# A chunk-pipelined mixer layer: the next chunk's x is loaded, measured, published and normalised at other steps

## What is computed

```
mod = silu(c) @ w_ada + b_ada;  shift, scale, gate = split(mod, 3)
h = layer_norm(x) * (1 + scale) + shift
proj = h @ w_in                                   # (2048,1024) @ (1024,2560)
xa, ga, u, v, gb = split(proj)                    # 512 channels each
ya = pool_mixer(xa) * silu(ga)                    # causal means over 2,4,8,16 tokens, a 128x128 map per group
yb = sgu_mixer(gelu(u), gelu(v)) * silu(gb)       # per 128 tokens and head: u * (W LN(v) + b)
y = concat(ya, yb) @ w_out                        # (2048,1024) @ (1024,1024)
z = alpha * x + gate * y
return layer_norm(z) * ln_g + ln_b
```

## Time and profile before

| what | value |
|---|---|
| three runs | 684.82, 684.26, 682.94 us, median 684.26 |
| profiled execution | 681.78 us, of which the span is 680.1 us |
| granted PE clock, mean | 0.990 |
| PE busy | 656.3 us (97%) |
| DVE busy | 496.2 us (73%) |
| ACT busy | 252.3 us (37%) |
| DMA queues of SP and ACT | 58.6% and 13.7% of 16 engines |

### The profile page before, as it was taken

The page is one execution under the profiler, slowest core; times in us unless marked ns, Lnnn a source line. Parts: engine busy times, 40 slices in busy tenths (PEclk is TensorE's granted clock), DMA queues, the critical chain, the costliest instruction groups (busy, mean ns, idle before and its releaser), DMA issues.

```text
span 680.1 us, 8503 instructions
## 1 busy us (share of the span) xinstructions
PE 656.3 (97%) x3055; PEld 546.0 (80%) x3055; DVE 496.2 (73%) x980; ACT 252.3 (37%) x335; POOL 51.1 (8%) x77
## 2 busy tenths in 40 slices
PE   8999999999989999989899999999999999999995
PEld 8888888877868888877688888888788888888884
DVE  5678897839979969539997757649997653436776
ACT  4424543316511332233673333242673332333300
POOL 2000100100002210000001210000001210000010
PEclk9999999998999999999899999999999999999999
DMA  8999776989399895997448995897549885654111
GB/s 337 359 344 360 260 280 249 287 217 355 102 323 379 289 409 195 215 347 275 153 157 288 320 314 178 147 371 270 161 149 315 299 317 193 207 166 141 64 63 62
DMA packets 52987, 168.62 MB, mean 248 GB/s; under 512 B 8621, under 2 KB 9681, under 8 KB 52946
## 3 DMA queue, kind: packets, MB, share of 16 engines
q1 hardware_dynamic: 44306, 136.63, 58.6%
q10 hardware_dynamic: 8640, 31.46, 13.7%
HBM read 139.75 MB, written 28.32 MB: 247 GB/s over the span
## 4 chain that ended last, share of the span: by engine, by line
PE 65%; DVE 15%; DMA 10%; issue 5%; ACT 3%; SPq 1%; ACTq 0%; POOL 0%; POOLq 0%; DVEq 0%
PE bank_b L1331 43%; PE bank_a L1331 16%; DMA w_float<-in_w_units 4%; DMA w_float<-xa_units 2%; DVE w_low L841 2%; DVE x_norm L868 2%; DMA token_rows<-x_rstd 2%; PE bank_a L1418 1%; PE bank_a L1458 1%; DMA out_units<-mod_spare 1%; PE bank_b L1391 1%; PE bank_a L1449 1%; ACT w_high L677 1%; DVE y_low L1064 1%; DVE mixed L1245 1%
## 5 line engine op out<-in xcount | busy, mean ns | idle before, releaser
L1331 PE MATMUL bank_b<-h_high,w_high 128*128 128x512 f32 x512 | 202.5, 395 | 2.2 <-issue 2.0
L1331 PE MATMUL bank_b<-h_high,w_low 128*128 128x512 f32 x512 | 199.6, 390 | 0.0
L1331 PE MATMUL bank_b<-h_low,w_high 128*128 128x512 f32 x512 | 199.5, 390 | 0.0
L677 ACT ACTIVATE w_high<-w_float 128x1024 fp32r<-128x1024 f32 x98 | 103.3, 1055 | 136.4 <-DMA w_float<-in_w_units 87.7
L1331 PEld LDWEIGHTS bank_b<-h_high,w_high 128*128 128x128 f32 x512 | 96.3, 188 | 22.5 <-issue 3.5
L1331 PEld LDWEIGHTS bank_b<-h_high,w_low 128*128 128x128 f32 x512 | 96.2, 188 | 20.0
L1331 PEld LDWEIGHTS bank_b<-h_low,w_high 128*128 128x128 f32 x512 | 96.3, 188 | 19.5 <-issue 0.5
L841 DVE TENSOR_TENSOR w_low<-w_float,w_high 128x1024 fp32r<-128x1024 f32 x38 | 46.3, 1220 | 12.8 <-ACT w_high L677 12.6
L613 POOL TENSOR_TENSOR z_rstd<-z_var_eps,minus_half 128x1 f32<-128x1 f32 x16 | 19.0, 1185 | 406.2 <-DVE z_var_eps L1162 199.4
L1331 PE MATMUL bank_a<-w_high,y_high 128*128 128x512 f32 x96 | 39.1, 408 | 7.4 <-DVE w_low L841 7.4
L1331 PE MATMUL bank_a<-w_high,h_high 128*128 128x512 f32 x96 | 38.1, 397 | 2.8 <-DVE tanh L1154 2.8
(11 more groups left out here) (223 smaller groups left out, 1037.1 us busy)
## 6 DMA issues: line engine op xcount, KB each, us to landing
w_float<-in_w_units SPq DMA_DIRECT2D x74, 512.0 KB, 5.3
w_low<-low_units ACTq DMA_DIRECT2D x60, 512.0 KB, 4.9
x_norm<-in_x SPq DMA_DIRECT2D x16, 512.0 KB, 6.3
low_units<-w_low SPq DMA_DIRECT2D x16, 512.0 KB, 7.7
z<-in_x SPq DMA_DIRECT2D x16, 512.0 KB, 6.0
w_float<-out_units SPq DMA_DIRECT2D x16, 512.0 KB, 4.1
out<-z SPq DMA_DIRECT2D x15, 512.0 KB, 6.3
z<-in_mod_units SPq DMA_DIRECT2D x12, 512.0 KB, 9.6
```

The lines of the kernel that those rows point to most:

```text
L677: nc.scalar.activation(w_of(c, n)[0], w_float(c, n), ACT.Copy).then_inc(w_high, 1)
L1331: last = mm(bank, wl if n == 2 else wh, ml if n == 1 else mh, start=start and n == 0, stop=stop and n == 2, skip_group_check=skip_group_check)
```

## The change

In chunks 1 and 2 the x tiles are loaded at steps 1 to 4 (6 to 9 before), measured at 5 to 8 (8 to 11), the rows stored at 9 (12), and the eight blocks normalised over steps 13 to 19 (two at each of 16 to 19). In chunk 0 the loads stay, the last two tiles are measured at 12 and 13 (14 and 15), and the rows stored at 14 (16). In every chunk the fetch of the rows stands three steps behind their store (one before), and chunk 0 too issues one x-by-channel load a step (four at once before). `sum_weights(1)` moves from the last step of chunk 0 to the first of chunk 1, and its stores one step on. No instruction is added or removed on PE, DVE, ACT or GpSimd. Nor is any DMA.

```diff
-SUMS_IN = {(0, 24): 0, (0, 27): 1, (1, 4): 2, (1, 9): 3}
-PREP_STORE_IN = {(0, 25): 0, (1, 1): 1, (1, 6): 2, (1, 11): 3}
+SUMS_IN = {(0, 24): 0, (1, 0): 1, (1, 4): 2, (1, 9): 3}
+PREP_STORE_IN = {(0, 25): 0, (1, 2): 1, (1, 6): 2, (1, 11): 3}
...
-FAST_X_ROWS_IN = 12
-FAST_X_CENTRE_IN = {16: (0, 1), 17: (2, 3), 18: (4, 5), 19: (6, 7)}
+FAST_X_ROWS_IN = 9
+FAST_X_CENTRE_IN = {13: (0,), 14: (1, 2), 15: (3,), 16: (4,), 17: (5,), 18: (6,), 19: (7,)}
+ROWS_BACK = 3
...
-                    if not last and 6 <= n < 6 + TILES:
-                        j = n - 6
+                    if not last and x_load_in(c) <= n < x_load_in(c) + TILES:
+                        j = n - x_load_in(c)
                         sp.wait_ge(h_high, (c + 1) * KT)
                         sp.dma_start(xn[:, j, :], x_tiles[c + 1, j]).then_inc(xn_landed[j], 16)
...
                     if not last and x_rows_in <= n < x_rows_in + TILES:
-                        for i in (n - x_rows_in,) if c in FAST else (range(TILES) if n == x_rows_in else ()):
-                            sp.dma_start(xT[:, 2 * i:2 * i + 2, :], x_channels[c + 1][:, 2 * i:2 * i + 2, :])\
-                                .then_inc(xT_landed[i], 16)
-                    if not last and n == x_rows_in + 1:
+                        i = n - x_rows_in
+                        sp.dma_start(xT[:, 2 * i:2 * i + 2, :], x_channels[c + 1][:, 2 * i:2 * i + 2, :])\
+                            .then_inc(xT_landed[i], 16)
+                    if not last and n == x_rows_in + ROWS_BACK:
                         sp.wait_ge(rows_stored, (c + 1) * 32)
```

More of the change, by code:

```diff
@@ L73 @@
 QUARTER = 256
-X_STATS_IN = {10: 0, 11: 1, 14: 2, 15: 3}
-X_ROWS_IN = 16
+X_LOAD_IN = 6
+X_STATS_IN = {10: 0, 11: 1, 12: 2, 13: 3}
+X_ROWS_IN = 14
 X_CENTRE_IN = {19: (0, 1), 20: (2, 3), 21: (4, 5), 22: (6, 7)}
 H_IN = {20: (0, 1), 21: (2, 3), 22: (4, 5), 23: (6, 7)}
-FAST_X_STATS_IN = {8: 0, 9: 1, 10: 2, 11: 3}
-FAST_X_ROWS_IN = 12
-FAST_X_CENTRE_IN = {16: (0, 1), 17: (2, 3), 18: (4, 5), 19: (6, 7)}
+FAST_X_LOAD_IN = 1
+FAST_X_STATS_IN = {5: 0, 6: 1, 7: 2, 8: 3}
+FAST_X_ROWS_IN = 9
+FAST_X_CENTRE_IN = {13: (0,), 14: (1, 2), 15: (3,), 16: (4,), 17: (5,), 18: (6,), 19: (7,)}
+ROWS_BACK = 3
 FAST_H_IN = {22: (0,), 23: (1,), 24: (2,), 26: (3,), 28: (4,), 29: (5,), 30: (6,), 32: (7,)}
@@ L380, in x_tables, with x_load_in @@
             return X_STATS_IN, X_ROWS_IN, X_CENTRE_IN, H_IN
+        def x_load_in(c):
+            return FAST_X_LOAD_IN if c in FAST else X_LOAD_IN
         def m_sem(m):
```

## The result

The changed kernel takes 668.65 us (668.01 to 669.73, four runs), the kernel before beside it 684.54 us (682.94 to 686.13, four runs): ratio 0.977, 95% interval 0.974 to 0.980. Forecast were 666.0 us and a range of 662.5 to 673.0. The profiled execution takes 668.01 us, of which the span is 666.3 (before 681.78 and 680.1).

The account below looks back on a forecast made before the run. PE was busy 97% of the span, so only idling and clock could be won: 4.7 + 3.9 + 2.0 + 6.5 + 2.0 = 19.1, less 1.0 = 18.1 us, giving 663.7 profiled, 666 as median; range 662.5 to 673.

Parts of the forecast that it names:

- The list of places: Seven PE idle records behind the set-up, in chunks 0 to 2, taken as all that can be won: 19.1 us.
- B: Start of chunk 1: 2.82 us of PE idling and 1.89 of clock, to go by moving the sums; 4.71 us.
- A: Between units 19 and 20 of chunk 0: 2.17 us of PE idling, 1.7 of clock, to go; 3.9 us.
- The hiding work: Chunk 1's start: five units of PE work (27 us) against some 20 of DVE cover DVE's 3 us lateness.
- C: Ahead of unit 16 of chunk 1: 2.03 us of PE idling, to go with the store at step 9.
- D: Units 21, 22 and 23 of chunk 1: idling of 0.73, 1.98 and 1.05 us, 6.5 with clock, to go.
- E: Unit 23 of chunk 2: 1.44 us of PE idling, 2.0 in all, to go by spreading the normalising.
- I charge 1.0 us for one of these in chunk 1: Units 13 and 14 of chunk 1, behind the moved row store: 1.0 us taken off the gain of 19.1.
- 18.0 us of room: Unit 12 of chunk 1: time from its low load's issue to its start, against a longest landing of 16.2 us.
- rival 1: Units 12 to 14, chunks 1 and 2: the store's dead stretch makes new waits, 7.8 us, so 673; chance 0.14.
- the trace agrees: ACT's low load took 16.2 us beside SP's store, read as agreeing with the skill's completion-order rule.

Follow-up runs that it names:

- the packed store: Changed kernel with each row store as 128 pieces of 16 bytes, not 512 of 4, and rows read in steps of four: 672.41 us, ratio 0.984.
- the layout alone: Kernel before with 16-byte row-store pieces and statistics tiles loaded with tokens 4p to 4p+3 on partition p, no step moved: 668.15 us, ratio 0.9855.

## Why the prediction was right, point by point

- **The list of places** held: all seven waits of the earlier trace rows are gone, and chunks 2 and 3 run at full pace. 19.1 us was a sound price for them: the trace gives 13.8 and the 5.0 of unit 13's stretch, 18.8.
- **B** was sized for PE as it came then. With A gone PE is earlier, so the move of the sums was worth 7.9 us at its place (5.98 and 1.94 when put back). Unseen in the sum, but without effect on it, since both places go. The hiding work was named rightly: the sums now run at 198.37 and delay nobody on PE.
- **A**: `w_high` of unit 21 ends at 148.4, forecast 147, and the gate rows at 150.4, forecast 149, which leaves 1.9 us and not 3. Unit 19's weights let ACT start at 139.45, forecast near 138. A sign named in the prediction did not come: ACT's idling for weights was to fall under 5 us, and it is 8.19 in chunk 0 and 7.20 in chunk 1.
- **C and D**: C went with the store's place. D is two things: about 1 us of idling from DVE's mass of blocks, the rest from the inputs that the store made late. The text had both, and the run with the blocks alone put back separates them.
- **E**: gone, 2.0 us forecast, 1.8 measured in chunk 2.
- **The step that was mis-sized** is "I charge 1.0 us for one of these in chunk 1". Unit 13 costs 4.7. The 18.0 us of room beside it are unit 12's, by the earlier trace rows; for units 13 and 14 the text has "1 to 3 us of room" and no row. Unit 13's load goes out at 262.94, behind ACT's 7.37 us of waiting for DVE, 5.7 us before PE wants it. It takes 8.6 us and is 3 us late. So rival 1's mechanism came, in one chunk of two, at 4.7 of its 7.8 us. Beside it the profiled run lies 4.3 us over the 663.7 of the sum, the median only 2.7 over 666, as profile and median of the changed kernel stand 0.6 us apart and not 2.5. That the median is so near is partly luck: this 1.9 us hides as much of the 4.3.
- **The sum of places is not a sum of parts.** What A and B win, chunk 1 partly takes back: 8.6 us by place, 3.9 by measurement, with or without the x part. The charge of 1.0 was the only term that stood for this. Beside the run with the sums put back, PE comes to unit 13 7.0 us earlier, while its load goes out at the same time (262.94 and 262.82); no term of the sum follows such a pair.
- **The loads beside the store.** They land late on both queues: SP's weight load issued just ahead of the store (252.08) took 10.8 us, and ACT's low part issued at 251.86 as long. Unit 13's low part on ACT's queue took 8.6 and 8.8 us, and 4.1 where it went out 2.9 us after the packed store was down (254.26 + 6.8 = 261.1). The Trainium skill, DMA: Bandwidth & Descriptors, Queues, rings and completion order, says that a transfer's completion increment waits for the earlier writes of its DMA engine, across queues. The store's own writes account for part of the lateness at most: the store was down at 252.93 + 13.2 = 266.1 and the load only at 271.5, and in the earlier trace rows the load landed 9.5 us after the store of the earlier trace rows, so "the trace agrees" means no more than that the load came down after the store. Between 266.1 and 271.5 the engines move 385 GB/s, so the load then shares them with what has piled up. Nor are they full while the store is in flight: with the sums put back, the window behind the store shows them 46% busy at 92 GB/s, and a low part that goes out at its start, at 252.2, takes 12.2 us:

```profile
252.00:265.00 13.00, 13.00 (x67) 11.07 (x66) 10.96 (x22) 4.81 (x8) 0.00 (x0) 1.00 0.46 92
```

What holds the engines back while the 4-byte store is in flight stays open; that its small pieces are the cause is shown by the packed store.

## What to carry to other kernels

Price idle places one by one, but ask of each what the engine meets next if it comes earlier: here a quarter of the gain (4.7 of 19.1 us) was waited again at unit 13 of chunk 1, in the stretch behind the row store, where the issue of a load didn't come earlier with PE. When several waits lead back to one small transfer, change the transfer before the schedule: the layout alone gave 10.6 us with no step moved, and on top of the new order it left PE without a wait. And count what a new layout does to each operation that reads it.

## What the runs showed of the hardware

- A store of 2 KB in 512 pieces of 4 bytes took 13.2 and 13.5 us to land in chunk 1, in 128 pieces of 16 bytes 6.8 us; the GB/s beside it rose from 182 to 257 while the busy share fell from 1.05 to 0.83. The pages count 52987 DMA packets and 50683: 2304 fewer, 384 for each of six stores.
- A vector operation on 128x512 fp32 with one input read 16 bytes apart took 1.08 us against 0.68. The Trainium skill, SBUF — State Buffer, Door 1: The DMA port swizzle, says that each new line of 16 bytes costs a penalty; the rows agree, but not with its "4 fp32" as a stride that is free.
- What a wait costs in pace behind it isn't a function of its length alone: 1.7 us behind 3.00 of idling and 1.9 behind 5.98, but 0.27 behind 2.14 (96 matmuls in 22.03), where the granted clock stays at 1.00. Behind a wait of 2.38 us, a window of the first packed kernel (rows read in steps) shows a granted clock of 0.57, near the lower of the two levels. First the kernel before with the layout alone, behind its 2.14 us, then that window:

```profile
197.00:220.00 23.00, 22.70 (x100) 18.85 (x101) 22.17 (x37) 4.46 (x6) 5.12 (x4) 1.00 1.00 381
...
325.00:329.00 4.00, 4.00 (x11) 3.11 (x11) 4.00 (x6) 4.00 (x6) 0.00 (x0) 0.57 0.74 232
```
